# Turning the FFN's gated product: 32x32 blocks on VectorE and SBUF transfers in place of TensorE transposes

## The reference, cut to what matters

```python
h2 = rms_norm(x, g_pre_ffn[l]) * (1 + scale_f) + shift_f
f = (jax.nn.silu(h2 @ w_ffn_gate[l]) * (h2 @ w_ffn_up[l])) @ w_ffn_down[l]
x = x + gate_f * rms_norm(f, g_post_ffn[l])
```

## Time and profile before

| | us |
|---|---|
| median of three runs | 2398.11 |
| span of the profiled execution | 2395.4 |
| runs' median less that span | 2.7 |
| TensorE busy in the span | 2379.1 |
| VectorE busy | 1594.5 |
| ScalarE busy | 1120.6 |

### The profile page before, as it was taken

One profiled execution on the slowest core, in us unless ns is written; L12 is line 12 of the kernel. 1 busy time (PEld: TensorE's weight loads), 2 busy tenths in 40 slices (PEclk: granted clock), 3 DMA queues, 4 the chain that ended last, 5 costly groups with the idle time before them and its releaser, 6 DMA issues.

```text
span 2395.4 us, 31219 instructions
## 1 busy us (share of the span) xinstructions
PE 2379.1 (99%) x11027; PEld 1973.6 (82%) x11027; DVE 1594.5 (67%) x1962; ACT 1120.6 (47%) x1415; POOL 9.8 (0%) x18
## 2 busy tenths in 40 slices
PE   8999999999999999999999999999999999999998
PEld 7888788888888888888888888888888888888887
DVE  7998899899787765444444465446654557777664
ACT  4544545544464444444444454445544444444554
POOL 0001000000000000000000000000000000000000
PEclk9999999999999999999999999999999999999999
DMA  9986479999768875555655555655555554444454
GB/s 392 384 313 209 155 265 352 331 343 366 294 202 273 281 245 192 188 180 197 207 193 193 193 193 180 210 201 184 201 192 187 183 194 158 148 167 155 157 190 159
DMA packets 148490, 539.32 MB, mean 225 GB/s; under 512 B 16768, under 2 KB 18080, under 8 KB 147744
## 3 DMA queue, kind: packets, MB, share of 16 engines
q1 hardware_dynamic: 145584, 528.28, 64.4%
q10 hardware_dynamic: 2800, 9.59, 1.1%
HBM read 535.69 MB, written 2.11 MB: 225 GB/s over the span
## 4 chain that ended last, share of the span: by engine, by line
PE 98%; DVE 1%; DMA 1%; ACT 0%; issue 0%; SPq 0%; ACTq 0%; DVEq 0%
PE acc L1970 29%; PE acc L1972 29%; PE acc L1971 29%; PE tb L2052 2%; PE tb L2509 1%; DMA start_raw<-in_wa_dram 1%; PE tb L1970 1%; PE tb L1971 0%; PE tb L1972 0%; PE acc L2022 0%; PE acc L2021 0%; PE acc L2020 0%; PE tb L2512 0%; PE tb L2239 0%; PE acc L2031 0%; DVE macc L1340 0%
## 5 line engine op out<-in xcount | busy, mean ns | idle before, releaser
L1149 DVE TENSOR_TENSOR lo<-raw,hi 128x1024 fp32r<-128x1024 f32 x809 | 968.2, 1208 | 596.8 <-ACT hi L566 595.0
L566 ACT ACTIVATE hi<-raw 128x1024 fp32r<-128x1024 f32 x809 | 842.1, 1049 | 900.4 <-PE acc L1972 705.5
L1970 PE MATMUL acc<-hi,Hh 128*128 128x512 f32 x1960 | 775.4, 396 | 1.2 <-DVE Hl L1692 0.7
L1972 PE MATMUL acc<-hi,Hl 128*128 128x512 f32 x1960 | 764.3, 390 | 0.0
L1971 PE MATMUL acc<-lo,Hh 128*128 128x512 f32 x1960 | 763.1, 389 | 0.0
L1970 PEld LDWEIGHTS acc<-hi,Hh 128*128 128x128 f32 x1960 | 368.1, 188 | 79.0 <-issue 4.4
L1972 PEld LDWEIGHTS acc<-hi,Hl 128*128 128x128 f32 x1960 | 367.9, 188 | 77.7
L1971 PEld LDWEIGHTS acc<-lo,Hh 128*128 128x128 f32 x1960 | 368.4, 188 | 75.5 <-issue 1.4
L1970 PE MATMUL acc<-hi,hbh 128*128 128x512 f32 x512 | 204.8, 400 | 0.0
L1972 PE MATMUL acc<-hi,hbl 128*128 128x512 f32 x512 | 200.1, 391 | 0.0
L1971 PE MATMUL acc<-lo,hbh 128*128 128x512 f32 x512 | 199.6, 390 | 0.0
(11 more groups left out here) (325 smaller groups left out, 1966.5 us busy)
## 6 DMA issues: line engine op xcount, KB each, us to landing
raw<-in_wa_dram SPq DMA_DIRECT2D x680, 512.0 KB, 4.3
late_raw<-in_wa_dram SPq DMA_DIRECT2D x96, 512.0 KB, 5.4
raw<-in_wb_dram SPq DMA_DIRECT2D x96, 512.0 KB, 3.4
start_raw<-in_wa_dram SPq DMA_DIRECT2D x64, 512.0 KB, 7.8
raw<-in_wc_dram SPq DMA_DIRECT2D x64, 512.0 KB, 4.2
x<-in_x_dram SPq DMA_DIRECT2D x2, 1024.0 KB, 6.1
gm<-gate_rows ACTq DMA_DIRECT2D x2, 1024.0 KB, 8.2
x<-in_x_dram ACTq DMA_DIRECT2D x1, 2048.0 KB, 9.2
```

Of the source, the lines that this page charges most:

```text
L566: act.activation(hi[:, s, 0:n], raw[:, r, 0:n], ACT.Copy).then_inc(hi_ready, 1)
L1149: dve.tensor_tensor(lo[:, s, 0:n], raw[:, r, 0:n], hi[:, s, 0:n].bitcast(F32), ALU.subtract)\
L1970: pe.matmul(dst(tt), a, hi[:, s, w], start=first and i == 0, stop=False)
L1972: mm = pe.matmul(dst(tt), b, hi[:, s, w], start=False, stop=last and i == kts - 1)
```

## The change

What is turned stays the same, and how it is turned changes:

- VectorE, after the two multiplications, waits until `tok[:, 0]` is written and issues two `transpose` instructions (one for each position half), which turn each 32x32 block within its 32 partitions, into `sgt`.
- SP gets `move_blocks(n)` for every tile: it waits for these blocks and issues 16 DMAs, SBUF to SBUF, of 32 partitions x 1 KB each (32 KB), which carry each block to its partitions in `tok[:, 0]`.
- ScalarE takes `hidh` from `tok[:, 0]` in SBUF after unit 22 (at 23), and VectorE `hidl` before unit 24, not at unit 20 from PSUM.
- TensorE's eight transposes for a tile go, with their waits for PSUM banks; before the down product's first and 21st unit it waits for `hid_split`.
- SP's stream is written out for the first five tiles and then looped with 16 loads and 16 moves a turn. `HID_BLOCKS_AT[n]` is unit 16n + 18: before the moves of tile n, SP issues every load up to four ring positions past what VectorE has consumed when it begins unit 16n + 18.

```diff
+HID_BLOCKS_AT = [FFN0 + 16 * n + 18 for n in range(FT)]
...
+        blocks_out = sgt[:].rearrange("p a (j m) -> p (a j) m", j=2)
+        blocks_in = tok[:, 0].rearrange("p a (i m) -> p (a i) m", i=2)
...
+            def move_blocks(n):
+
+                sp.wait_ge(hid_blocks, n)
+                for i in range(4):
+                    for j in range(4):
+                        sp.dma_start(blocks_in[32 * j:32 * j + 32, i, :], blocks_out[32 * i:32 * i + 32, j, :])\
+                            .then_inc(hid_turned, 16)
...
-            stream(wa, RING_MODS + FFN0, STREAM)
+            first = RING_MODS + FFN0
+            for n in range(FFN_MOD):
+                upto = HID_BLOCKS_AT[n] + sum(unit < HID_BLOCKS_AT[n] for unit in MODS) + RING
+                while c.n["unit"] < upto:
+                    load(wa[RING_MODS + c.n["unit"]])
+                move_blocks(n + 1)
+            first = RING_MODS + c.n["unit"]
+            with c.loop(sp, FT - FFN_MOD, unit=16) as n:
+                for j in range(16):
+                    load(wa[bass.ds(n * 16 + (first + j), 1)].rearrange("a p n -> (a p) n"))
+                move_blocks(n + (FFN_MOD + 1))
+            stream(wa, RING_MODS + c.n["unit"], STREAM)
...
+            def hidden_hi(n, turned):
+
+                act.wait_ge(hid_turned, turned)
+                for tt in range(TT):
+                    act.activation(hidh[:, cols(n * 4, 4), tt * P:(tt + 1) * P].rearrange("p k (i t) -> p k i t", i=4),
+                                   turned_half(tt), ACT.Copy).then_inc(hid_hi, 1)
...
-                split(8)
-                take_hi_tile(hidh, n * 4)
+                split(11)
...
-            def hidden(n, units=16):
-                split(units - 2)
+            def hidden(units=10):
+                split(units)
                 tile_done(2)
                 for tt in range(TT):
-
                     dve.tensor_tensor(tok[:, 0, tt, :], acc[:, 2 + tt, :], sgt[:, tt, :], ALU.mult).then_inc(acc_free[2 + tt], 1)
-                split(2)
-                take_lo_tile(hidl, hidh, n * 4)
+                n = c.up("hidden")
+                for tt in range(TT):
+
+                    dve.wait_ge(acc_free[2 + tt], n + (TILES_BEFORE_OUT // 2 + 3))
+                for tt in range(TT):
+                    ins = dve.transpose(blocks_out[:, :, tt * P:(tt + 1) * P].rearrange("p j (k t) -> p j k t", k=4),
+                                        tok[:, 0, tt, :].rearrange("p (k j c) -> p j k c", k=4, j=4))
+                ins.then_inc(hid_blocks, 1)
+                split(6)
...
-                def hidden():
-
-                    read_out(1)
-                    transpose_tok(0, tr_split)
-
-                tile(Hh, Hl, 0, 8, after={1: hidden})
+                tile(Hh, Hl, 0, 8)
                 tile(Hh, Hl, 1, 8)
```

More of the change, by code:

```diff
@@ L367, in two_blocks @@
         tr_copy = sem("tr_copy")
+        hid_blocks = sem("hid_blocks")
+        hid_turned = sem("hid_turned")
+        hid_hi = sem("hid_hi")
+        hid_split = sem("hid_split")
         uv_summed = sem("uv_summed")
@@ L437, in part_at, with turned_half @@
             return z[:, tt, (part - 4) * N:(part - 3) * N]
+        blocks_out = sgt[:].rearrange("p a (j m) -> p (a j) m", j=2)
+        blocks_in = tok[:, 0].rearrange("p a (i m) -> p (a i) m", i=2)
+        def turned_half(tt):
+            return blocks_in[:, :, tt * P:(tt + 1) * P].rearrange("p i (k t) -> p k i t", k=4)
         block = ctx.enter_context(nc.Block())
@@ L906, in _, with hidden @@
                 split(1)
-            def hidden(n, first=8):
+            def hidden_hi(n, turned):
[3 more added lines that the diff above has]
+                                   turned_half(tt), ACT.Copy).then_inc(hid_hi, 1)
+            def hidden(first=5):
                 split(first)
@@ L910, in hidden @@
                 read_out(lambda tt: sgt[:, tt, :], 0, ACT.Silu)
-                split(8)
-                take_hi_tile(hidh, n * 4)
-            hidden(0, FFN0 + 12 - c.n["unit"])
+                split(11)
+            hidden(FFN0 + 12 - c.n["unit"])
             for n in range(1, FFN_MOD):
-                hidden(n)
-            with c.loop(act, FT - FFN_MOD, unit=16, raw=16, split=2) as n:
-                hidden(n + FFN_MOD)
+                hidden_hi(n - 1, 256 * n)
+                hidden()
+            with c.loop(act, FT - FFN_MOD, unit=16, raw=16) as n:
+                hidden_hi(n + (FFN_MOD - 1), n * 256 + 256 * FFN_MOD)
+                hidden()
+            hidden_hi(FT - 1, 256 * FT)
             store_gate(1)
-            split(4)
+            split(1)
             load_gate(gm2, 1)
@@ L1710, in _, with hidden_lo @@
                 split(1)
-            def hidden(n, units=16):
-                split(units - 2)
+            def hidden_lo(n, taken):
+                for tt in range(TT):
+                    dve.wait_ge(hid_hi, taken + tt + 1)
+                    at = slice(tt * P, (tt + 1) * P)
+                    four = lambda ap: ap.rearrange("p k (i t) -> p k i t", i=4)
+                    ins = dve.tensor_tensor(four(hidl[:, cols(n * 4, 4), at]), turned_half(tt),
+                                            four(hidh[:, cols(n * 4, 4), at].bitcast(F32)), ALU.subtract)
+                ins.then_inc(hid_split, 1)
+            def hidden(units=10):
+                split(units)
                 tile_done(2)
@@ L1718, in hidden @@
                     dve.tensor_tensor(tok[:, 0, tt, :], acc[:, 2 + tt, :], sgt[:, tt, :], ALU.mult).then_inc(acc_free[2 + tt], 1)
-                split(2)
-                take_lo_tile(hidl, hidh, n * 4)
-            hidden(0, FFN0 + 20 - c.n["unit"])
+                n = c.up("hidden")
+                for tt in range(TT):
+                    dve.wait_ge(acc_free[2 + tt], n + (TILES_BEFORE_OUT // 2 + 3))
+                for tt in range(TT):
+                    ins = dve.transpose(blocks_out[:, :, tt * P:(tt + 1) * P].rearrange("p j (k t) -> p j k t", k=4),
+                                        tok[:, 0, tt, :].rearrange("p (k j c) -> p j k c", k=4, j=4))
+                ins.then_inc(hid_blocks, 1)
+                split(6)
+            hidden(FFN0 + 18 - c.n["unit"])
             for n in range(1, FFN_MOD):
-                hidden(n)
+                hidden_lo(n - 1, TT * (n - 1))
+                hidden()
             add_bias(GATE_F, KD)
             gated_gain(GATE_F, "g_post_ffn")
-            with c.loop(dve, FT - FFN_MOD, unit=16, raw=16, hi=2) as n:
-                hidden(n + FFN_MOD)
+            with c.loop(dve, FT - FFN_MOD, unit=16, raw=16, hidden=1) as n:
+                hidden_lo(n + (FFN_MOD - 1), n * TT + TT * (FFN_MOD - 1))
+                hidden()
+            hidden_lo(FT - 1, TT * (FT - 1))
             for t in range(3):
-                split(FK // 2 - (t == 0))
+                split(FK // 2 - (5 if t == 0 else 0))
                 gated_tile(fmix, gm2, t % 2, t * N)
@@ L2401, in _ @@
                 next_hidden()
-            with c.loop(pe, FT - FFN_MOD, unit=16, raw=16, acc0=1, acc1=1, tb0=1, tb1=1):
+            with c.loop(pe, FT - FFN_MOD, unit=16, raw=16, acc0=1, acc1=1):
                 next_hidden()
[L2405 to L2408, removed]
             for t in range(4):
                 if t == 0:
-                    tile(hidh, hidl, 0, FK // 2, before={FK // 2 - 2: split_now}, after={1: last_hidden})
+                    tile(hidh, hidl, 0, FK // 2, before={i: (lambda n=n: pe.wait_ge(hid_split, n)) for i, n in ((0, FT - 1), (FK // 2 - 2, FT))},
+                         after={1: lambda: gate_rows_out(1)})
                 elif t < 3:
```

## The result

The changed kernel takes 2464.4 us (median of four runs, 2461.9 to 2465.0) against 2397.7 us, the kernel before's median with a fourth run added to its three: slower by 66.7 us, a ratio of 1.0276 (95% interval 1.0264 to 1.0289). I had forecast 2419, between 2396 and 2436. The sign and the place were right, the size was not. The profiled execution's span went from 2395.4 to 2463.2 us.

A forecast was written before the change was run, and what follows sets the result against it. TensorE, busy for 2379.1 of 2395.4 us, was taken to bound the kernel. Transposes saved -10.0, stalls +26.4 and clock +4.8 sum to +21.2 us, 2416.6, plus 2.7 for the runs' median: 2419 us, range 2396 to 2436.

The forecast's parts named there:

- TensorE's gain: In eleven FFN tiles, removing eight transposes saves TensorE 0.91 us each, 10.0 us in all.
- VectorE: After the multiplications, which start at g: 1.35 us for two block transposes, blocks ready at g + 2.8, in time.
- Which load is late, and where: Behind the moves on SP's queue: unit 20's weight load in four loaded tiles, unit 22's in seven plain ones.
- The landing: The weight load queued behind the moves lands 3.6 us after its issue, at g + 14.1.
- the split of the late unit: After its load lands, ScalarE needs 1.06 and VectorE 1.2 us, 2.5 with handovers: ready at g + 16.6.
- An issue: On SP's queue, moves are issued 0.47 us apart, so a tile's sixteen hold the queue for 7.5 us.
- My own formula: TensorE's stall in a loaded tile is 16i - 1.64 us for issue interval i; plain tiles have none below 0.44.
- the stalls: TensorE waits 5.9 us in each of four loaded tiles (with `w_mod` loads), 0.4 in each of seven plain: 26.4 us.
- The clock: After each of four loaded-tile stalls TensorE may resume at half clock, costing 1.2 us each, 4.8 us in all.
- Cheap moves: Rival: a move costs SP's queue 0.10 us or less, no load is late, 2388 us; chance 0.17.
- The queue stays behind: Rival: loaded tiles' ring recovers only by tile end, or landings take 4.6 us with full clock cost; 2435 us, chance 0.15.

The follow-up runs named there:

- eight moves: The changed kernel with only eight of each tile's sixteen block moves (columns j = 0 and 1), half the blocks not moved: 2409.7 us.
- the hold alone: The kernel before, its TensorE transposes kept, with sixteen small SBUF-to-HBM transfers a tile added to SP's queue that nobody waits for: 2418.1 us.
- moves spread: The changed kernel with weight loads put between small groups of the moves on SP's queue, and hidh and hidl taken at units 26 and 27: 2393.6 us.

## Why the prediction was wrong

- *TensorE's gain*, 10.0 us: right. The kernel without the moves is 8.9 us faster.
- *VectorE*: 1.35 us for the pair of block transposes, 1.30 measured; blocks ready at g + 2.8, and it was g + 2.7.
- *Which load is late, and where*: right. Behind the moves stands the load of unit 20 in a loaded tile and of unit 22 in a plain one; eleven pauses, four long and seven short.
- *The landing*, 3.6 us, was 3.62; the split of the late unit 2.4 us against 2.5.
- *An issue*: **this is the step that failed.** "I take i = 0.47, with 0.33 below." It was 0.629 us (10.06 / 16), above both of my ends. I had thought about the number of partitions, and even expected fewer to be quicker, but the rows I leaned on the earlier trace rows were all transfers with HBM at one end, and the moves have SBUF at both. I had seen that no row was of that kind, and counted it only for the rival that an issue is cheaper. My own formula with 0.63 gives pauses of 16 x 0.63 - 1.64 = 8.4 us and 10.1 - 7.1 = 3.0 us. Measured from start to start they were 8.1 in the tile shown (7.9 idle and what the modelled end of a matmul hides) and 3.0. So the stalls were 53 us in place of 26.4, which alone takes the forecast from 2419 to 2446 us, past its range.
- *The clock*, the second term that was too small: that it falls was right, how often and at what price was not. I priced four long stalls at 1.2 us each, a guess between nothing and 2.4, and none of the plain tiles' stalls, which I had at 0.4 us, far below the 4.1 us without matmuls of the earlier trace rows. All eleven paid: in the plain tile a pause of 2.8 us was followed by half clock until 1056. The price was about 10.8 - 8.1 = 2.7 us in a loaded tile and 4.7 - 3.0 = 1.7 in a plain one, 4 x 2.7 + 7 x 1.7 = 23 us in place of 4.8. TensorE's rows give the same another way: 116 matmuls after the eleven pauses started about 0.43 us after the one before and not 0.23. The rule I cited from the Trainium skill (TensorE: Matmul & The Clock Gate, "Why this matters for your kernels"), that gaps between bursts of matmuls throttle the array, agrees with all eleven. It is not the whole: after pauses of 3.0 us (eight moves), 3.1 and 2.7 us (the hold alone) the clock did not fall, and after one of 2.0 us (moves spread) it did. What decides it for pauses of 2 to 3 us is not shown by these runs.

The sum again, with the measured sizes: -10 + 4 x 8.1 + 7 x 3.0 + 23 = +66 us; measured in the spans +67.8. The steps account for the loss.

- *The rivals.* Cheap moves: excluded by the issues. "The queue stays behind" had the right total nearest, with the wrong mechanism: within a tile the ring caught up after one pause, as I had said. The range ended at 2436 because I let the issue vary only downward from its row. The sentence from the Trainium skill (DMA: Bandwidth & Descriptors, "Issuing engines are not separate DMA queues") that the sequencer's time is usually small relative to the DMA does not hold for these moves: 0.63 us of queue against 1.9 to landing, and sixteen in a row cost 10 us.

What is not settled: where the loaded tiles' last short pauses come from when the moves are spread or on GpSimd's queue. ScalarE waits there for weight loads, with the DMA engines busy for four fifths of the time; whether it is the moves' share of those engines, the 1.3 us by which the block transposes delay the next load, or (with the moves spread) the 1.2 us for which each pair of moves holds that load back was not tried. The kernel without moves has those transposes and no pause, so they alone don't do it; its DMA engines were busy for a share of 0.80 there, against 0.83 and 0.82.

## What to carry to other kernels

Price a DMA in a queue by what its issue keeps behind it, not by its bytes: count the issues, take the interval from rows with the same memories at both ends, and ask which load is next in that queue and how many ring positions it is ahead. Where a burst of small transfers shares a queue with a prefetch stream, put each load that is due ahead of the next few of them, and take their result late. And price a pause of TensorE with what the clock costs after it: in the changed kernel a pause of 3 us cost 4.7, though in two of the others three pauses of about that length cost no more than themselves.

## What the runs showed of the hardware

- Back-to-back issues on SP's queue are 0.46 to 0.48 us apart from HBM to SBUF (32 KB, 32 or 128 partitions), 0.46 from SBUF to HBM (4 KB, 32 partitions), and 0.63 to 0.64 from SBUF to SBUF, whatever the size (4 to 32 KB) and the partitions (16 to 128). Single issues of 1.2 to 1.5 us turn up among them. GpSimd issued the same moves 0.49 us apart, but they landed 4.8 us after the issue, against 1.9 from SP's queue in one burst and 2.9 from SP's queue between weight loads.
- TensorE's granted clock fell to 0.50 during or up to 1 us after the changed kernel's eleven pauses, of 2.7 to 8.6 us, and stood there until 2.9 to 6.1 us after the matmuls had resumed. In other kernels it fell after a pause of 2.0 us and not after three of 2.7 to 3.1.
- A block transpose of 128x512 float32 on VectorE takes 0.69 us, as long as a two-input operation of that shape with one input in PSUM.
